# Two attentions, probabilities transposed inside the next weight slab

## The reference

```python
# first block: 8 query heads, 2 key heads, 64 wide; each block of 128 queries sees its own and the previous 128 keys
logits = einsum(q, k) * 64 ** -0.5 + bias
m = max(max(logits), sink);  p = exp(logits - m)
probs = p / (sum(p) + exp(sink - m));  out = einsum(probs, v)
merged = sigmoid(g_attn) * (out @ w_attn_branch) + sigmoid(g_ssm) * y_ssm

# second block: 16 query heads, 4 key heads; each block of 128 queries sees the blocks before, at and after it
scores = einsum(q * 64 ** -0.5, k) - slope * abs(dist)
... the same softmax with a sink; o = einsum(p / denom, v)
uc = conv4(u) + b           # u = xn @ w: the "u2" slabs, even ones
y_a = rg_lru(uc) * gelu(g_lru)   # g_lru = xn @ w: the "u2" slabs, odd ones
```

## Time and profile before

| | us |
|---|---|
| median of 3 runs | 1446.49 |
| lowest, highest | 1446.08, 1447.52 |
| the profiled execution's span, first to last instruction | 1443.7 |
| TensorE busy in it | 1407.0 |
| VectorE busy | 893.8 |
| ScalarE busy | 619.9 |

### The profile page before, as it was taken

The page is one execution under the profiler, slowest core; times in us unless marked ns, Lnnn a source line. Parts: engine busy times, 40 slices in busy tenths (PEclk is TensorE's granted clock), DMA queues, the critical chain, the costliest instruction groups (busy, mean ns, idle before and its releaser), DMA issues.

```text
span 1443.7 us, 17492 instructions
## 1 busy us (share of the span) xinstructions
PE 1407.0 (97%) x7100; PEld 1135.3 (79%) x7100; DVE 893.8 (62%) x1313; ACT 619.9 (43%) x987; POOL 1.9 (0%) x7
## 2 busy tenths in 40 slices
PE   6999999999999999999999999999999999999997
PEld 5776777787788888887787777778888888888886
DVE  7989864747635354354668888479964443453446
ACT  5473563424322222133336787788652321331232
POOL 0000000000000000000000000000000000000000
PEclk9999999999999999999999999999999999999999
DMA  5212224231333333333132111323233333233223
GB/s 197 88 59 89 60 73 132 74 123 53 95 100 96 107 89 103 88 91 102 56 102 73 45 59 59 103 73 102 88 103 102 88 103 97 93 102 103 88 88 102
DMA packets 37583, 131.60 MB, mean 91 GB/s; under 512 B 4432, under 2 KB 6608, under 8 KB 37248
## 3 DMA queue, kind: packets, MB, share of 16 engines
q1 hardware_dynamic: 37152, 127.16, 29.0%
q0 software_dynamic: 352, 3.34, 0.6%
HBM read 128.39 MB, written 2.10 MB: 90 GB/s over the span
## 4 chain that ended last, share of the span: by engine, by line
PE 84%; DVE 8%; ACT 6%; issue 2%; DMA 0%; SPq 0%; DVEq 0%; ACTq 0%
PE gp L1591 23%; PE gp L1593 23%; PE gp L1592 23%; PE mp L1797 2%; PE mp L1808 2%; PE mp L1775 2%; ACT w_hi L480 2%; DVE w_lo L913 1%; PE mp L1687 1%; PE mp L1689 1%; PE mp L1688 1%; PE mp L1591 1%; PE mp L1592 1%; PE mp L1593 1%; PE mp L1749 0%
## 5 line engine op out<-in xcount | busy, mean ns | idle before, releaser
L1591 PE MATMUL gp<-h_hi,w_hi 128*128 128x512 f32 x944 | 371.0, 393 | 12.8 <-DVE w_lo L913 10.9
L1593 PE MATMUL gp<-h_hi,w_lo 128*128 128x512 f32 x944 | 368.6, 390 | 0.0
L1592 PE MATMUL gp<-h_lo,w_hi 128*128 128x512 f32 x944 | 368.5, 390 | 0.0
L913 DVE TENSOR_TENSOR w_lo<-raw,w_hi 128x1024 fp32r<-128x1024 f32 x202 | 246.5, 1222 | 125.5 <-ACT w_hi L480 125.1
L480 ACT ACTIVATE w_hi<-raw 128x1024 fp32r<-128x1024 f32 x202 | 211.6, 1051 | 137.3 <-PE gp L1593 77.3
L1591 PE MATMUL gp<-a_hi,w_hi 128*128 128x512 f32 x652 | 256.1, 393 | 2.2 <-DVE w_lo L913 1.6
L1592 PE MATMUL gp<-a_lo,w_hi 128*128 128x512 f32 x652 | 253.9, 389 | 0.0
L1593 PE MATMUL gp<-a_hi,w_lo 128*128 128x512 f32 x652 | 253.9, 389 | 0.0
L1591 PEld LDWEIGHTS gp<-h_hi,w_hi 128*128 128x128 f32 x944 | 177.8, 188 | 53.0 <-issue 14.1
L1593 PEld LDWEIGHTS gp<-h_hi,w_lo 128*128 128x128 f32 x944 | 177.8, 188 | 37.3
L1592 PEld LDWEIGHTS gp<-h_lo,w_hi 128*128 128x128 f32 x944 | 177.9, 188 | 36.3
(11 more groups left out here) (293 smaller groups left out, 1652.6 us busy)
## 6 DMA issues: line engine op xcount, KB each, us to landing
raw<-slabs SPq DMA_DIRECT2D x202, 512.0 KB, 3.5
arena<-slabs SPq DMA_DIRECT2D x30, 512.0 KB, 3.6
arena<-x_in SPq DMA_DIRECT2D x4, 512.0 KB, 6.6
arena<-x_in POOLq DMA_DIRECT2D x1, 2048.0 KB, 8.7
out_t<-arena SPq DMA_DIRECT2D x8, 256.0 KB, 2.2
arena<-bias POOLq DMA_DIRECT2D x1, 1024.0 KB, 5.3
arena<-s5b SPq DMA_DIRECT2D x1, 512.0 KB, 9.5
arena<-s5c SPq DMA_DIRECT2D x1, 512.0 KB, 10.3
```

Source lines behind the costliest of these rows:

```text
L913: TT(w_lo[:, n % RING, :], raw(n), w_hi[:, n % RING, :].bitcast(F32), ALU.subtract).then_inc(w_lo_ready, 1)
L1591: pe.matmul(dst, hi, x_hi(t), start=t == 0, stop=False)
L1592: pe.matmul(dst, hi, x_lo(t), start=False, stop=False)
L1593: ins = pe.matmul(dst, lo, x_hi(t), start=False, stop=t == tiles - 1)
```

## The change

Three orders are changed, no instruction is added or taken away.

- **TensorE**: the transposes of unit u move into slab u+1. `turned(u, x)` does the key block x after the slab's tile 3, 4 or 6 (`TURN_AT`). `scores(u+2)` comes after the slab, and the values product of u after that. At the last unit of `att1`, which has no slab to follow, the transposes stand alone as before. In `att2` the last unit's transposes go into the first `mix` slab.
- **VectorE**: `logits` is divided into `masked` (the additions) and `maxima`. The order is now masks of u+2, inverse sums and scaling of u+1, maxima of u+2, `between`.
- **ScalarE**: `split` comes before the copies of the transposed probabilities, where it stood after the exponentials and the third copy.

```diff
+        TURN_AT = [3, 4, 6]
...
                     if u:
                         take_outputs(u - 1)
+                    if u + 1 < n:
+                        split(slab0 + u + 1 + AHEAD)
                     probs_t(u, slice(0, 2))
                     if u + 1 < n:
                         exponentials(u + 1)
                     probs_t(u, slice(2, 3))
                     if u + 1 < n:
-                        split(slab0 + u + 1 + AHEAD)
                         gate(u + 1)
...
                     if u + 2 < n:
-                        logits(u + 2)
+                        masked(u + 2)
                     if u + 1 < n:
                         inverse_sums(u + 1)
                         scaled_probs(u + 1)
+                    if u + 2 < n:
+                        maxima(u + 2)
+                    if u + 1 < n:
                         between(u + 1)
...
+                def turned(u, x):
+                    g, j, _ = A.chunks[u][x]
+                    if x == 0:
+                        pe.wait_ge(probs_ready, A.u0 + u + 1)
+                    if g >= 2:
+                        pe.wait_ge(pt_ready, g - 1)
+                    for h in range(4):
+                        ins = pe.transpose(mp[:, 3 + g % 2, h * P:(h + 1) * P],
+                                           A.logit[u % 2][:, h, j * P:(j + 1) * P], ident)
+                    ins.then_inc(pt_done, 1)
+
                 for u in range(n):
                     b, pp, _ = A.units[u]
-                    pe.wait_ge(probs_ready, A.u0 + u + 1)
-                    for x, (g, j, kb) in enumerate(A.chunks[u]):
-                        if x == 2 and u + 2 < n:
-                            scores(u + 2)
-                        if g >= 2:
-                            pe.wait_ge(pt_ready, g - 1)
-                        for h in range(4):
-                            ins = pe.transpose(mp[:, 3 + g % 2, h * P:(h + 1) * P],
-                                               A.logit[u % 2][:, h, j * P:(j + 1) * P], ident)
-                        ins.then_inc(pt_done, 1)
-                    if u + 2 < n and len(A.chunks[u]) < 3:
+                    some = range(len(A.chunks[u]))
+                    if u + 1 < n or not A.name:
+                        between(u + 1, {TURN_AT[x]: lambda u=u, x=x: turned(u, x) for x in some})
+                    else:
+                        for x in some:
+                            turned(u, x)
+                    if u + 2 < n:
                         scores(u + 2)
-                    between(u + 1)
                     if u:
                         pe.wait_ge(*((h_lo_ready, H_AT["y1"] + u) if A.name else (at_copied, u)))
                     for x, (g, j, kb) in enumerate(A.chunks[u]):
```

More of the change, by code:

```diff
@@ L1159, in attention, with masked @@
             def attention(A, between, first=None):
-                def logits(u):
-                    row, L = mini[u % 3], A.logit[u % 2]
+                def masked(u):
+                    L = A.logit[u % 2]
                     b, pp, hp = A.units[u]
@@ L1174, in logits, with maxima @@
                                 in1=sc, op0=ALU.mult, op1=ALU.add).then_inc(lane_read, 1)
+                def maxima(u):
+                    row, L = mini[u % 3], A.logit[u % 2]
+                    b, pp, hp = A.units[u]
+                    lo, hi = A.span(u)
                     dve.wait_ge(lane_read, 4 * (A.u0 + u) + 4)
@@ L1207, in attention @@
                 n = len(A.units)
-                logits(0)
+                masked(0)
+                maxima(0)
                 if first:
@@ L1212, in attention @@
                 scaled_probs(0)
-                logits(1)
+                masked(1)
+                maxima(1)
                 between(0)
@@ L1832, in _ @@
             transpose_values(att1)
-            attention(att1, lambda u: a_stage("gate_s", u) if u < len(att1.units) else None)
+            attention(att1, lambda u, then={}: a_stage("gate_s", u, then=then))
             outputs(CT - 1)
@@ L1893, in values2, with mix_slab, inputs2 @@
                 transpose_values(att2)
-            def mix_slab(key):
-                gemm("mix", MIX_SLAB[key] - SLAB["mix"], 8, 1, h, hl, first=MIX_GATES.index(key))
-            def inputs2(u):
+            def mix_slab(key, then={}):
+                gemm("mix", MIX_SLAB[key] - SLAB["mix"], 8, 1, h, hl, first=MIX_GATES.index(key), then=then)
+            def inputs2(u, then={}):
                 if u == 0:
@@ L1901, in inputs2 @@
                 if u < len(att2.units):
-                    gemm("u2", u, 8, 1, h, hl, then={2: values2} if u == 0 else {})
+                    gemm("u2", u, 8, 1, h, hl, then={2: values2} if u == 0 else then)
                 else:
                     pe.wait_ge(lane_read, 4 * (att2.u0 + len(att2.units)))
-                    mix_slab(STAGE[0])
+                    mix_slab(STAGE[0], then)
             attention(att2, inputs2, begin2)
```

## The result

The changed kernel takes **1456.26 us** (median, 1454.73 to 1458.20) where the kernel before takes 1446.86 on the same chip (1446.08 to 1447.52). The measured ratio is 1.0071, with a 95% interval of 1.0060 to 1.0082: slower by 9.4 us by the medians and by some 10 us by the ratio, which is not simply the quotient of two medians. The forecast was 1453.4, with a range of 1450.0 to 1457.2. One execution of experiment 4 ran in a slower state (1771.34 us, mean granted clock 0.75) and is left out of its median.

The account below looks back on a forecast made before the run. TensorE, busy 97% of the span, was taken as the bound. Its own gain of 2.1, new waits of 9.0 and `att1`'s 0 gave +6.9: span 1450.6, plus 2.8 outside it, 1453.4 us; range 1450.0 to 1457.2.

Parts of the forecast that it names:

- Part 1: TensorE's own work in `att2`: units get shorter with the transposes inside the slab, a gain of 2.1 us.
- 8 units with two key blocks: Units of `att2` with two key blocks: each gains 0.15 us of TensorE's work, from 8.78 to 8.63.
- Part 2: `att2`: ScalarE reads each slab too late for the next one, 15 new TensorE waits, together 9.0 us.
- the second's stand 0.90 later: ScalarE's chain in Part 2: second key block's transposes at 3.75 us after the slab's start, 0.90 behind the first's.
- Part 3: `att1`: gains per unit and from the scaling wait offset 1.1 to 1.2 lost at the end: 0, within 0.5.
- Part 4: VectorE and ScalarE's split: probabilities ready with 0.6 to 1.0 us of slack; split costs nothing; convolution may delay `a_hi` 0.1 to 0.2.
- The probabilities are late as well: Rival: in `att2`, units with three key blocks also wait inside the slab, about 1457 us; chance 0.09.
- Only the work moves: Rival: copies start sooner, ScalarE's chain is shorter, waits vanish, 1444.4 us; chance 0.11 together with half of this.
- The rule on table loads: Skill's drain of about 1380 ns per table switch, 14 waits longer by 19 us in all, 1473; chance 0.01.

Follow-up runs that it names:

- experiment 4: Changed kernel with Tanh in place of Gelu in the gate of `y_a`, so `att2` switches no table: 1445.88 us, ratio 1.0004 to the kernel before.
- experiment 2: Changed kernel with the transposes one tile later, behind tiles 4, 5 and 7: 1468.64 us, ratio 1.0152 to the kernel before.
- experiment 5: Changed kernel with an odd slab read ahead of `a_hi` on ScalarE: 1452.13 us, ratio 1.0050 to the kernel before.
- experiment 6: Changed kernel with ScalarE's split back at its old place, behind the exponentials and third copy: 1473.52 us, ratio 1.0197 to the kernel before.
- experiment 3: Changed kernel with the transposes one tile earlier, behind tiles 2, 3 and 5: 1452.22 us, ratio 1.0040 to the kernel before.
- experiment 7: Changed kernel with transposes behind tiles 2, 3 and 5 and an odd slab read before `a_hi`: 1447.04 us, ratio 1.0007 to the kernel before.
- experiment 1: Changed kernel with TensorE's order of before, keeping the new ScalarE and VectorE orders: 1446.15 us, ratio 1.0001 to the kernel before.
- experiment 8: As experiment 7, with `att2` unit 0's transposes between slabs 0 and 1, `att1`'s last exponentials ahead of copies: 1444.42 us, ratio 0.9996 to the kernel before.

## Why the prediction was right, and where it was off

**The mechanism.** As forecast: TensorE, busy for 97% of the time, had to wait for ScalarE's reading, since the chain behind the transposes was moved into the slab. Experiments 2, 5 and 6 lengthen or shorten this chain by a known piece and the time follows (3 does until the convolution stops it); 4 and 7 take it below TensorE's unit and the loss is gone. The forecast had 15 waits and there are 15 places: 11 shown as waits for line 546, and four as the 0.26 pause inside the values product. For those four I had a wait of about 0.15 for the reading; what was late was the third copy, one step ahead of it. The pattern holds too: 1.11 and 0.59 where two key blocks follow one another (forecast 1.06 and 0.52), 0.70 and 0.26 in the middle (0.69 and 0.15), 0.78 between slabs 0 and 1 (0.94).

**Two terms of the sum were mis-sized**, and both made it 3 us too low for `att2`.

- *Part 1, TensorE's own gain: -2.1 forecast, -0.4 measured* (experiment 4). In its timeline a unit without waits takes 10.00 us with three key blocks, where it took 10.02 (forecast 9.91), and 8.67 with two, where it took 8.77 (forecast 8.63). A group of four transposes in a slab costs exactly the 0.44 of the earlier trace rows: 828.69 - 827.79 = 0.90. But the pace of the matmuls around them is 0.231 rather than 0.228, which over a slab is the missing 0.08. And two of the "8 units with two key blocks", the last two, have no scores; from values product to values product they took 7.49 and now 7.61 and 7.64. For them I had written a gain where there is a loss of 0.12 and 0.15.
- *Part 2, the waits: +9.0 forecast, some +10.3 measured* (9.92 + 0.4). Shown are 8.7 in the waits and 4 x 0.26 in the pauses, 9.7; the rest is about 0.04 at each place, more than the idle time that the row shows. The step that failed is "the second's stand 0.90 later (0.44 + two or three paces)". Between the two groups stand three matmuls, not two: 829.16 - 828.02 = 1.14. That makes 14 chains 0.24 longer, +3.4. It was partly made good by three others: the copy starts 829.79 - 829.16 = 0.63 behind the transposes, not 0.70 (-1.0), TensorE is itself ready later by 0.09 or 0.04 (-0.9), and the wait between slabs 0 and 1 is 0.78, not 0.94 (-0.2). 9.0 + 3.4 - 1.0 - 0.9 - 0.2 = 10.3.

That 1456.26 still lies in the range is in part luck: the upper end was put at 1457.2 for late probabilities, which did not come, and not for these two terms.

The copy behind these transposes, on ScalarE's timeline of the changed kernel:

```profile
829.79 0.60 ACT L657 ACTIVATE arena<-mp 128x512 f32<-128x512 f32 x1 [0.54 <-PE mp L1807]
830.41 1.28 ACT L635 ACT_TABLE_LOAD   x1
831.71 0.20 ACT L635 ACTIVATE arena<-arena 128x4 f32<-128x4 f32 x1
```

**Part 3, `att1`: 0 forecast, +0.54 measured.** The end on TensorE's timeline, before the change:

```profile
213.34 1.08 PE L1808 MATMUL mp<-arena 128*64 128x256 f32 x8
214.36 1.09 PE L1797 MATMUL mp<-par,arena 128*128 128x128 f32 x8
215.79 1.08 PE L1808 MATMUL mp<-arena 128*64 128x256 f32 x8 [0.34 <-ACT arena L656]
```

And now:

```profile
215.30 1.08 PE L1826 MATMUL mp<-arena 128*64 128x256 f32 x8
217.63 1.09 PE L1807 MATMUL mp<-par,arena 128*128 128x128 f32 x8 [1.25 <-DVE arena L1204]
219.10 1.08 PE L1826 MATMUL mp<-arena 128*64 128x256 f32 x8 [0.37 <-DVE h_lo L1211]
```

The first wait is the one that was named, 1.25 for "1.1 to 1.2". The second, 0.37, costs next to nothing: the last values product stood for 0.34 before too, for the copy, and comes 1.47 behind its transposes where it came 1.43. What ends this wait is another thing now, VectorE's writing of an earlier unit's output (`h_lo`), which has been pushed back behind the scaling. From one values product to the next the end takes 3.80 where it took 2.45, a loss of 1.35, some 0.2 more than put down. The larger error lies in the gain. Up to unit 6's values product `att1` takes 215.30 - 151.25 = 64.05 where it took 213.34 - 148.48 = 64.86: 0.81 gained, and 0.14 for each of 7 units and the 0.5, less 0.1 to 0.2 at the first slab, would have been 1.3. Three units in a row gained 0.10 each, and the last one, without scores, lost 0.12.

**Part 4.** Right. VectorE had the probabilities ready at every transpose in a slab, with a tile to spare by experiment 3, and the split ended ahead of the first copy. The 0.1 to 0.2 that was kept for the convolution was not needed in this kernel: in the unit above its last step, from 842.38 on for 0.75 us, ends 0.4 before `a_hi` starts at 843.51. It was needed in experiment 3.

**The rivals.** *The probabilities are late as well* would show waits at the transposes in a slab; there is none. *Only the work moves* needed copies that start 1.1 us sooner; they start 0.07 sooner. The size of the work's gain, which also carried this rival, was a fifth of what I gave it. So even had the waits vanished, the kernel would have stood at 1446 to 1447, as experiments 4 and 7 do, and not at 1444.4.

**The rule on table loads.** In the odd chain above the load starts at 844.15, 0.02 after the end of `a_hi`, takes 1.28, and the reading starts at 845.44; in the even one 830.41 + 1.28 = 831.69, and the exponential starts at 831.71. The Trainium skill ("ScalarE: Activation LUTs", What ACT_TABLE_LOAD costs) adds a drain of some 1380 ns to each switch. The trace of this kernel has no room for it, before or after, and the measurement decides. The changed kernel's 1456.26 is also far from the 1473 of that rule. Experiment 4 alone would not decide it: the waits of up to 1.13 would be gone with either price.

## What to carry to other kernels

Work that is moved to a place where it "costs TensorE nothing" takes its whole chain along: follow it through the engine behind it to the next thing that TensorE needs from that engine, and compare with the length of one period; here a cover of 3.6 us was cut to less than zero. If the chain is a few tenths too long, shorten it at its own engine (the reading ahead of `a_hi`, the split ahead of the copies), since each tenth counts once per unit. And when a distance between two moved items decides, count the instructions between them one by one in the order as built: one matmul of 0.23 us missed there was the larger error of this forecast's waits.

## What the runs showed of the hardware

**Short falls of TensorE's clock behind waits.** In experiment 2, TensorE's timeline behind the 1.82 us wait reads:

```profile
896.39 0.47 PE L1603 MATMUL gp<-h_hi,w_hi 128*128 128x512 f32 x1 [1.82 <-ACT arena L546]
...
898.01 0.63 PE L1603 MATMUL gp<-h_hi,w_hi 128*128 128x512 f32 x1
898.43 0.63 PE L1604 MATMUL gp<-h_lo,w_hi 128*128 128x512 f32 x1
...
900.57 0.63 PE L1603 MATMUL gp<-h_hi,w_hi 128*128 128x512 f32 x1
900.99 0.44 PE L1604 MATMUL gp<-h_lo,w_hi 128*128 128x512 f32 x1
```

From 898.01 to 900.99 the matmuls start 0.43 apart rather than 0.23, the lower of the clock's two levels (1.2 GHz). The view by windows shows the granted clock of these stretches, the number before the last two of each line:

```profile
895.00:900.00 5.00, 3.61 (x11) 2.96 (x12) 4.30 (x9) 2.46 (x4) 0.00 (x0) 0.77 0.12 14
900.00:905.00 5.00, 5.00 (x28) 3.94 (x27) 0.00 (x0) 2.31 (x3) 0.00 (x0) 0.89 0.26 94
```

Eight starts at 0.20 more each are 1.6 us. In experiment 6 the three waits of 2.06 to 2.07 in `att2` (slabs at 787.35, 900.90 and 923.99) are each followed by such a stretch, and its waits of 1.66 and less in `att2` by none; in experiment 2 the waits of 1.79 by none. In the changed kernel no wait in `att2` is over 1.13, and its clock is 1.00 there throughout. So a wait can cost almost its own length once more, and experiments 2 and 6 came out above a sum of waits alone by about these falls.

It isn't certain either. Every one of these kernels has one wait of 2.05 or 2.06 us near 383 us of the span, far from both attentions. In five of the ten profiled executions the lower level followed it, among them the kernel before, whose rows follow, and in five it didn't, among them the changed one:

```profile
383.13 0.57 PE L1611 MATMUL mp<-h_hi,w_hi 128*128 128x512 f32 x1 [2.05 <-DVE h_lo L957]
383.50 0.63 PE L1612 MATMUL mp<-h_lo,w_hi 128*128 128x512 f32 x1
383.92 0.63 PE L1613 MATMUL mp<-h_hi,w_lo 128*128 128x512 f32 x1
```

Nor does the length of the wait decide it alone. Near 687 us of the changed kernel a fall follows a wait of only 1.31 (the next matmul, at 689.48, starts 0.43 after the last one shown):

```profile
687.26 1.05 PE L1645 MATMUL mp<-par,arena 128*128 128x1 f32 x8 [1.31 <-DVE arena L929]
...
689.05 0.63 PE L1603 MATMUL gp<-h_hi,w_hi 128*128 128x512 f32 x1
```

In experiment 1 the same wait of 1.31 (to 686.71) is followed by none. What decides it stays open.

Executions of one and the same kernel differ with it. Of the 21 of the kernel before that stand beside experiments 5 to 8, the three with a mean granted clock of 0.998 took 1442.78 to 1443.94 us, the twelve with 0.996 1445.45 to 1446.64, and the four with 0.993 1447.31 to 1448.94. Such a step is about as large as what experiment 8 stands below the kernel before.
